# Cached pages of a decoder step: score pages issued by GpSimd, value pages by SyncE

## What is computed

```python
def mla_sample(q_nope, q_pe, ckv, kpe, pool_ckv, pool_kpe, layer_idx, page_table, w_ukv):
    ...
    q_lat = jnp.einsum('bshn,chn->bshc', q_nope, w_uk)
    ckv_past = pool_ckv[layer_idx, page_table].reshape(db, -1, A_KV_LORA)
    kpe_past = pool_kpe[layer_idx, page_table].reshape(db, -1, A_ROPE)
    sc_past = (jnp.einsum('bshc,btc->bhst', q_lat, ckv_past)
               + jnp.einsum('bshr,btr->bhst', q_pe, kpe_past)).astype(jnp.float32) * SM_SCALE
    ...
    p = jax.nn.softmax(jnp.concatenate([sc_past, sc_self], axis=-1), axis=-1).astype(ckv.dtype)
    o_lat = (jnp.einsum('bhst,btc->bshc', p[..., :n_past], ckv_past)
             + jnp.einsum('bhst,btc->bshc', p[..., n_past:], ckv))
```

## Time and profile before

| | us |
|---|---|
| median of 3 runs | 2278.7 |
| lowest, highest | 2274.31, 2280.89 |
| profiled execution | 2275.55 |
| its span | 2273.9 |

### The profile page before, as it was taken

How to read it: one execution, slowest core, us unless ns; L and a number is a source line. 1 busy time by engine, 2 the same in 40 slices (tenths; PEclk the granted TensorE clock), 3 DMA queues, 4 the chain that set the end, 5 groups by cost and what they waited for, 6 DMA issues and landing times.

```text
span 2273.9 us, 46824 instructions
## 1 busy us (share of the span) xinstructions
PE 2171.1 (95%) x18285; PEld 2065.0 (91%) x18285; DVE 1036.7 (46%) x2004; ACT 733.8 (32%) x1297; POOL 122.1 (5%) x230
## 2 busy tenths in 40 slices
PE   8999999999775889999999999999999999999997
PEld 8999999997443458999999999999999999999997
DVE  5444344367653344544434344443446664444333
ACT  6222223353222333422223242222332233222222
POOL 0000000001234340000000000000000000000000
PEclk9999999999987899999999999999999999999999
DMA  4222232244899872222223222222222222222232
GB/s 163 92 92 92 93 100 96 83 129 141 223 268 293 231 216 89 84 92 92 92 93 100 95 93 92 92 90 95 99 89 100 90 87 93 92 91 86 96 99 74
DMA packets 101037, 261.98 MB, mean 115 GB/s; under 512 B 14385, under 2 KB 49218, under 8 KB 100866
## 3 DMA queue, kind: packets, MB, share of 16 engines
q1 hardware_dynamic: 89746, 228.83, 31.8%
q0 software_dynamic: 11184, 31.69, 4.8%
HBM read 255.29 MB, written 5.16 MB: 115 GB/s over the span
## 4 chain that ended last, share of the span: by engine, by line
PE 61%; DVE 1%; issue 1%; ACT 0%; DMA 0%; DVEq 0%; POOLq 0%; ACTq 0%; POOL 0%
PE bank L281 20%; PE bank L280 20%; PE bank L282 20%; PE bank L1988 0%; DMA sb_v_raw<-in_cache 0%; PE bank L305 0%; DVE sb_x L1040 0%; PE bank L2002 0%; DVE sb_x L375 0%; ACT L314 0%; PE bank L1980 0%; PE bank L1755 0%; ACT sb_t L345 0%; DVE sb_h_lo L353 0%; ACT sb_h_hi L340 0%
## 5 line engine op out<-in xcount | busy, mean ns | idle before, releaser
L280 PE MATMUL bank<-sb_h_hi,sb_w_hi 128*128 128x260 f32 x3552 | 1006.1, 283 | 9.5 <-DVE sb_h_lo L1523 8.1
L281 PE MATMUL bank<-sb_h_lo,sb_w_hi 128*128 128x260 f32 x3552 | 1007.1, 284 | 0.0
L282 PE MATMUL bank<-sb_h_hi,sb_w_lo 128*128 128x260 f32 x3552 | 1003.8, 283 | 0.0
L252 ACT ACTIVATE sb_w_hi<-sb_raw 128x1024 fp32r<-128x1024 f32 x339 | 359.3, 1060 | 1261.5 <-PE bank L282 1257.6
L280 PEld LDWEIGHTS bank<-sb_h_hi,sb_w_hi 128*128 128x128 f32 x3552 | 668.7, 188 | 11.1 <-DVE sb_w_lo L258 8.2
L282 PEld LDWEIGHTS bank<-sb_h_hi,sb_w_lo 128*128 128x128 f32 x3552 | 671.5, 189 | 0.0
L281 PEld LDWEIGHTS bank<-sb_h_lo,sb_w_hi 128*128 128x128 f32 x3552 | 668.2, 188 | 0.2
L258 DVE TENSOR_TENSOR sb_w_lo<-sb_raw,sb_w_hi 128x1024 fp32r<-128x1024 f32 x339 | 415.3, 1225 | 381.1 <-ACT sb_w_hi L252 380.4
L281 PE MATMUL bank<-sb_a_lo,sb_w_hi 128*128 128x260 f32 x1408 | 399.1, 283 | 0.0
L280 PE MATMUL bank<-sb_a_hi,sb_w_hi 128*128 128x260 f32 x1408 | 398.7, 283 | 0.0
L282 PE MATMUL bank<-sb_a_hi,sb_w_lo 128*128 128x260 f32 x1408 | 397.7, 282 | 0.0
(11 more groups left out here) (283 smaller groups left out, 1572.7 us busy)
## 6 DMA issues: line engine op xcount, KB each, us to landing
sb_raw<-in_w SPq DMA_DIRECT2D x339, 512.0 KB, 3.5
sb_s_raw<-in_cache SPq DMA_DIRECT2D x256, 144.0 KB, 5.0
sb_v_raw<-in_cache POOLq DMA_DIRECT2D x192, 128.0 KB, 5.8
sb_v_raw<-in_cache SPq DMA_DIRECT2D x64, 128.0 KB, 7.1
sb_x<-in_x SPq DMA_DIRECT2D x4, 520.0 KB, 6.2
out_y<-sb_x SPq DMA_DIRECT2D x8, 260.0 KB, 2.3
sb_st<-in_state POOLq DMA_DIRECT2D x8, 256.0 KB, 8.0
out_state_s<-sb_st POOLq DMA_DIRECT2D x8, 256.0 KB, 7.3
```

Of the source, the lines that this page charges most:

```text
L252: nc.scalar.activation(w_hi[slot][:], raw[slot][:], ACT.Copy).then_inc(S("w_hi_done"), 1)
L280: nc.tensor.matmul(out, wh, xh, start=first and c == 0, stop=False)
L281: nc.tensor.matmul(out, wh, xl, start=False, stop=False)
L282: mm = nc.tensor.matmul(out, wl, xh, start=False, stop=last and c == chunks - 1)
```

## The change

Score pages of quads 1 to 31 are issued by GpSimd, all value pages by SyncE. Quad 0's score pages stay where they were. Each kind now has one semaphore for each half of its ring, and one more for the first score quad, which another queue issues than those after it. GpSimd calls `pages_to` at the same places as before, but `pages_to` runs up to the score slot, so it starts with quad 1 and waits for `s_done`. The state loads and stores and the memsets stay at their places of GpSimd's program. SyncE's first value quad waits for the start of the query projection, the second for `q_lat_mm`, the others for `v_done`.

```diff
         def loaded(kind, k):
-            by = "_sp" if kind == "v" and k % COLG == COLG - 1 else ""
-            return S(f"{kind}_loaded{k // COLG % 2}{by}")
+            return S("s_loaded_first" if kind == "s" and k < COLG else f"{kind}_loaded{k // COLG % 2}")
...
         def quad_loaded(eng, kind, q):
 
             uses = q // 2 + 1
-            if kind == "s":
-                eng.wait_ge(loaded("s", COLG * q), 16 * JOB * COLG * uses)
-            else:
-                eng.wait_ge(loaded("v", COLG * q), 16 * JOB * (COLG - 1) * uses)
-                eng.wait_ge(loaded("v", COLG * q + COLG - 1), 16 * JOB * uses)
+            if kind == "s" and q:
+                uses = (q + 1) // 2
+            eng.wait_ge(loaded(kind, COLG * q), 16 * JOB * COLG * uses)
...
             load(n_cache - 3)
             load(n_cache - 2)
 
-            sp.wait_ge(S("half_done"), 2 * U0["ukv"])
-            for k in range(COLG, S_JOBS + LAG):
-                if k < S_JOBS:
-                    if k % 4 == 0:
-                        numbers = page_numbers(sp, k, 4)
-                    load_job(sp, "s", k, numbers[k % 4])
-                if k >= LAG and (k - LAG) % 4 == 3:
-                    if k - LAG == RING - 1:
-                        sp.wait_ge(S("q_lat_mm"), 1)
-                    load_job(sp, "v", k - LAG, page_numbers(sp, k - LAG, 1)[0])
+            for k in range(S_JOBS):
+                if k % COLG == 0:
+                    numbers = page_numbers(sp, k, COLG)
+                if k == 0:
+                    sp.wait_ge(S("half_done"), 2 * U0["uq"])
+                if k == COLG:
+                    sp.wait_ge(S("q_lat_mm"), 1)
+                load_job(sp, "v", k, numbers[k % COLG])
             load(n_cache - 1)
...
-            quads = [0]
+            quads = [1]
 
             def pages_to(end):
 
-                while quads[0] < S_JOBS // COLG and COLG * quads[0] + LAG - 5 < end:
-                    numbers = page_numbers(pool, COLG * quads[0], 3)
-                    for j in range(3):
-                        load_job(pool, "v", COLG * quads[0] + j, numbers[j])
+                while quads[0] < S_JOBS // COLG and COLG * quads[0] - 5 < end:
+                    numbers = page_numbers(pool, COLG * quads[0], COLG)
+                    for j in range(COLG):
+                        load_job(pool, "s", COLG * quads[0] + j, numbers[j])
                     quads[0] += 1
...
             pool.wait_ge(S("half_done"), 2 * U0["uq"])
             pool.dma_start(w_uk[:], dram["w_uk"]).then_inc(S("w_uk_loaded"), 16)
-            pages_to(LAG - 4)
             pool.wait_ge(S("ckv_stored"), 16)
+            pool.wait_ge(S("half_done"), 2 * U0["ukv"])
+            pages_to(4)
             pool.wait_ge(S("q_s_ready"), Q_S_STEPS)
             state_in(0)
             state_in(1)
```

## The result

The changed kernel takes **2287.9 us** in the median of 8 runs (2282.64 to 2296.53); the kernel before takes 2278.9 us beside it. The ratio is 1.0047, with a 95% interval of 1.0035 to 1.0059: it is slower, by 9.0 us between the medians and 10.7 us by the ratio. The forecast of 2273 us had the wrong sign, and its range (to 2286 us) missed the median by 2 us. Timed again on another occasion the change gave 2285.7 us, ratio 1.0040 (1.0022 to 1.0058). Over both occasions its 15 runs have a median of 2286.5 us.

What follows compares the result with a forecast made beforehand. Full DMA engines at 605 to 680 us were taken to bound that stretch, inside one TensorE chain. Terms 0 + 2.7 - 6.6 - 1.5 = -5.4 us took the profiled 2275.55 to 2270.1, as a median 2273 us; range 2262 to 2286.

Steps and rivals of the forecast that it cites:

- What bounds the kernel: DMA engines are full at 605 to 680 us; one TensorE chain carries gains or losses there whole to the end.
- Packed stretch: 605 to 680 us: dearer packets cost 1.3 us, vanished score waits gain 1.3; net 0 us, between -5 and +6.4.
- The upper bound: Packed stretch: at 459 GB/s, read as the software queue alone, a quad costs 0.46 us more, at most +6.4 us.
- The start: Memsets behind quad 2 end at 571.8 us, second scores come 4.5 us late; +2.7 us, between 0 and +4.5.
- The state stage: From 683.5 us: quad 17 ahead of the states loses its 4.6 us wait, quad 18 keeps 3.6; -6.6 us with stores.
- The last four state stores: Stores that left at 727.27 us behind value pages would leave a little earlier: -1 us, between -3 and +1.
- The late part: The 2.89 us score wait at 818.6 us should go, value pages may give half back: -1.5 us, between -3 and +4.
- Rival 3: Value pages become the late ones at 600 to 720 us, row by row behind 3 KB packets: 2288 us, chance 0.25.
- GpSimd held up at issue: GpSimd's delayed issue would now hit score pages; its DMAs lasted 536 to 643 ns, so the effect was called small.
- Rival 2: Queue order does nothing, pages land after 7.0 and 7.1 us on either; only the start's +2.7 stays: 2281 us, chance 0.15.

Runs made afterwards that it cites:

- The loads alone: Kernel of only the page loads, no compute, seven phases of queue mixes; eight quads took 65.7 us in the mix of before, 60.8 in the change's.
- early start kernel: Changed kernel, but GpSimd issues only score quad 1 before state loads and memsets, quad 2 after; 2281.27 us, ratio 1.0022; again 2281.13 us, 1.0014.
- late start alone: Kernel before, but GpSimd waits for the first scores and issues value quad 1 before the two state loads and memsets; 2281.65 us, ratio 1.0013.

## Why the prediction was wrong, point by point

**What bounds the kernel.** Right as far as the rows show: the DMA engines are full in this stretch in every kernel, and gains and losses there arrive at the end (+9.5 us at the output projection, +9.0 us in the span of the same execution).

**Packed stretch, 0 us.** The working was wrong in two places that nearly cancel. Software packets of score pages hold three rows, not two, so a quad needs eight packets fewer on each engine than I had, and by my own line (0.052 ns a byte, 15 ns a packet) about the same 8.4 us as before. The loads alone confirm that the quad isn't dearer. The upper bound misread its row: the slice of 459 GB/s (532.75 to 532.875 us) wasn't the software queue alone, ten of its 19 packets and most of its bytes were the hardware queue's. What I left out is that the share of each queue changes whom TensorE waits for: value waits at 671.76 us and before it, 5.4 us in four waits up to 680 us. From quad 7 to quad 16 the lag grew by 2.9 us, from 8.9 to 11.8. The middle of the estimate was near; its gain of 1.3 us for vanished score waits was paid back by value waits.

**The start, +2.7 us, at most +4.5.** This step failed. The order of GpSimd's work and the end of the memsets were right (571.8 forecast, 571.41 seen, with quad 1's wait of 5.26 us where I wrote "about 4"). The discount was wrong: I let TensorE's 1.79 us wait for VectorE absorb a part. But VectorE's next instruction is the reduction of exactly those scores, so VectorE stood for 7.29 us, and the reduction and its state steps came 5.6 us later; the wait for it was still 1.50 us. A wait for an engine that itself waits for the late thing is no slack. A second cost was put at nothing: behind the wait of 4.6 to 5.3 us the second scores took 2.79 us, at a granted clock of 0.50, in all three profiles with a late start, and 1.48 us in all ten with an early one. The lag was 5.7 us at quad 1 (4.3, plus the 1.4 by which this execution was early) and grew to 9.6 at quad 6 by the same reckoning, where TensorE's clock was lower (last section). Taking the start away gave back 5.4 us of median, twice the 2.7 of this term.

**The state stage, -6.6 us.** This step failed too, and by more. Quad 17's wait did go. But the issue times were those of a program that keeps its pace: quad 17 at 678.7 us, as SyncE had it, and the states right behind. In the early start kernel GpSimd issued quad 17 at 682.40 and the states 7 us later than before, 3.3 us of it lag and 3.23 us the pause without a named releaser; in the changed kernel the states left at 694.17, 10.7 us later. So quad 18 waited 10.08 and 9.71 us in the two profiles of the early start kernel where I had 3.6. In the changed kernel the place shows two value waits and a score wait, 8.58 us together, against 9.24 us before. The gain was nil. I had counted the waits of one kind only: with quad 18 put ahead of states 4 to 7 its wait fell to 4.64 us and the value pages' rose to 5.69. The last four state stores, which I expected a little earlier, left at 738.18 us, 10.9 us later than before, about the lag of that place. ScalarE's wait at `sb_k_t` is now ended by TensorE (6.56 us) and not by the stores; that moved nothing that can be measured.

**The late part, -1.5 us.** The score wait of 2.89 us is 1.04 us in the second profile, with 0.97 us of value wait behind it; in the first, 2.49 and 3.28. From quad 19 to quad 31 the lag went from 13.3 to 10.2 us. The step stands, within its range.

**The rivals.** Rival 3 (value pages become the late ones, 2288 us) is near what happened: 2286.5 us. The range that I gave ended at 2286, under the middle of this rival, though it had a chance of 0.25. Its mark, TensorE's value waits over 10 us, is there: 11.7 and 19.6. Its arithmetic was partly wrong: it put +6.4 on dearer packets, which the loads alone refute, and 4.5 on the start, which was nearer 5.4. So its time came out in part by luck. The rest is the assignment of the kinds, 3.3 us, whose way into the time is argued and not shown, and a state stage without its gain. Its last point, GpSimd held up at issue, stays untested: one page DMA of the changed kernel lasted up to 809 ns, where 512 is usual, and the pauses of 3.2 to 3.3 us are unexplained. Rival 2 (landing doesn't depend on the queue) falls by the queues alone: 6.7 us on one and 8.8 to 13.4 on the other. The section of the Trainium skill on which it leaned (DMA: Bandwidth & Descriptors, Issuing engines are not separate DMA queues) says that issuing from several engines saves sequencer time only. For the bytes in total the trace nearly agrees (274, 302 and 292 GB/s); for which page comes first it doesn't, with both queues full. The row that misled me was 7.0 beside 7.1 us in the earlier trace rows: the fourth value job, 8.5 us on SyncE's queue, stood under it, and it was the only comparison of the queues with the same kind of page. That row was in the profile before the run and I didn't weigh it.

I gave the change a chance of 0.25 to lose. What would have raised it is to follow the score pages' new queue through its blocked instructions: each of the three moves (memsets behind quad 2, states behind quad 17, all value rows in the smallest packets) can take slack from something else, and the first two could be read from rows.

## What to carry to other kernels

Before counting an engine's wait as slack, look whether the engine that it waits for will itself be held by the late event. Before moving an urgent load to a program that also carries other loads, write down the issue time of everything behind it, because a page that waits for its buffer blocks them all. Where two queues fill the DMA engines, count the bytes in a packet of each: here the queue with the larger packets got more of the bytes, the other kind became late, and the total stayed. And where the engines are full, add up the waits for both kinds before counting one as a gain.

## What the runs showed of the hardware

The software queue (issued by GpSimd) joined rows: packets of 4.6 KB on average, three rows of 1.5 KB, and of 4.1 KB, four rows of 1 KB. The hardware queue sent a packet for each row. With both queues full the engines took 1.6 hardware packets for each software packet, in both mixes. The Trainium skill (DMA: Bandwidth & Descriptors, Queues, rings and completion order) describes a round over the queues, a packet each, a packet there being a group of descriptors. The counts agree in kind, since shares go by packets and not by bytes, and differ in size, 1.6 to 1; no run shows whether a packet of the profile is one of the page's.

GpSimd needs 512 ns to issue a score page and 536 ns a value page; SyncE 317 and 333 ns. Alone on the software queue value pages were bound by this issue: GpSimd issued all 64 without a pause in 33.8 us, the DMA share was 0.81, and pages landed 2.5 us after issue. Score pages were issued without a pause too, but there the DMA share was 0.97, so both limits were near.

TensorE's granted clock fell in some executions where the engine had only its usual short waits. In the stretch 580 to 605 us (windows view: after the busy times the clock, the DMA share and GB/s), for the kernel before, for the early start kernel (first profile) and for the kernel before with the late start alone:

```profile
580.00:605.00 25.00, 16.39 (x205) 9.29 (x198) 15.77 (x49) 7.81 (x20) 3.22 (x6) 1.00 0.73 214
```

```profile
580.00:605.00 25.00, 16.38 (x203) 9.40 (x195) 15.55 (x47) 7.81 (x20) 13.87 (x28) 1.00 0.67 190
```

```profile
580.00:605.00 25.00, 19.11 (x182) 10.23 (x174) 14.27 (x42) 7.75 (x19) 0.00 (x0) 0.80 0.57 170
```

The changed kernel's second profile has the clock and TensorE time of the third row (0.80 and 19.11 us). Of thirteen profiles, the three with a late start (both of the change, and the late start alone) had 0.80 to 0.86 here, so part of the stretch ran at 1.2 GHz; of the ten with an early start five had 1.00 and five 0.80 to 0.84. The same four matrix products took 1.13 us at the higher level (2.4 GHz) and 1.44 to 2.08 us where it fell. Where the clock fell here, late start or early, TensorE's lag grew by 1.8 to 2.8 us from quad 4 to quad 6. So a late start costs its own wait and 1.3 us on the second scores, and may cost this much more behind them, but an early start doesn't keep the clock: these runs can't say what decides it. It may be a part of why the one profile of the late start alone shows +9 us where the median moved by 3.
